# Two levels of an HGRN head's score matrix from products on VectorE and matrices of ones on TensorE

## What is computed

```
def hgrn2_chunk_scan(q, k, v, log_f):
    b = jnp.cumsum(log_f, axis=2)
    diff = b[:, :, :, None] - b[:, :, None, :]
    dec = jnp.where(mask, jnp.exp(jnp.where(mask, diff, 0.0)), 0.0)
    att = jnp.einsum('bnthk,bnshk,bntshk->bnhts', q, k, dec)
    o_intra = jnp.einsum('bnhts,bnshv->bnthv', att, v)
...
    o = hgrn2_chunk_scan(qh, k_f, vh, a_f) + \
        flip(hgrn2_chunk_scan(flip(qh), flip(k_b), flip(vh), flip(a_b)))
```

## Time and profile before

| | |
|---|---|
| median of 3 runs | 1494.94 us |
| profiled execution | 1494.7 us |
| its span | 1492.9 us |
| TensorE (PE) busy | 1468.7 us, 98%, 11148 matmul records |
| VectorE (DVE) busy | 1069.0 us, 72% |
| ScalarE (ACT) busy | 803.8 us, 54% |
| granted TensorE clock | 0.997 of full speed |
| share of the chain that ended last on TensorE | 95% |

### The profile page before, as it was taken

The page is one execution under the profiler, slowest core; times in us unless marked ns, Lnnn a source line. Parts: engine busy times, 40 slices in busy tenths (PEclk is TensorE's granted clock), DMA queues, the critical chain, the costliest instruction groups (busy, mean ns, idle before and its releaser), DMA issues.

```text
span 1492.9 us, 27955 instructions
## 1 busy us (share of the span) xinstructions
PE 1468.7 (98%) x11148; PEld 1397.0 (94%) x11148; DVE 1069.0 (72%) x1818; ACT 803.8 (54%) x1721; POOL 90.6 (6%) x109
## 2 busy tenths in 40 slices
PE   7999999999999999999999999999999999999996
PEld 7999999999999999999999999999998889999984
DVE  7777777777664777777677777777786657777755
ACT  6555545655434555665555555556554446655542
POOL 0000000000000000000000000000001000000100
PEclk9999999999999999999999999999999999999998
DMA  5112111111213222222132121212112232222221
GB/s 208 60 55 71 58 58 57 58 57 58 86 58 100 73 72 72 72 72 72 57 100 85 59 69 59 70 57 71 57 58 86 71 100 72 74 84 79 79 78 64
DMA packets 34625, 109.94 MB, mean 74 GB/s; under 512 B 4928, under 2 KB 5056, under 8 KB 34496
## 3 DMA queue, kind: packets, MB, share of 16 engines
q1 hardware_dynamic: 34496, 108.15, 23.1%
HBM read 97.38 MB, written 2.10 MB: 67 GB/s over the span
## 4 chain that ended last, share of the span: by engine, by line
PE 95%; DVE 2%; ACT 1%; issue 1%; DMA 0%; DVEq 0%; SPq 0%; ACTq 0%
PE proj L1441 66%; PE pair L1510 8%; PE meta L1620 4%; PE pair L1605 2%; PE pair L1607 2%; PE main L1634 2%; PE meta L1622 1%; PE main L1575 1%; PE main L1576 1%; PE pair L1556 1%; PE main L1488 1%; PE main L1517 1%; PE pair L1563 1%; PE main L1579 1%; PE pair L1542 0%
## 5 line engine op out<-in xcount | busy, mean ns | idle before, releaser
L1441 PE MATMUL proj<-u_hi,w_hi 128*128 128x264 f32 (+1 forms) x2048 | 495.3, 313 | 8.7 <-DVE w_lo L1003 7.8
L1441 PE MATMUL proj<-u_hi,w_lo 128*128 128x264 f32 (+1 forms) x2048 | 465.6, 299 | 0.0
L1441 PE MATMUL proj<-u_lo,w_hi 128*128 128x264 f32 (+1 forms) x2048 | 465.5, 299 | 0.0
L1441 PEld LDWEIGHTS proj<-u_hi,w_hi 128*128 128x128 f32 x2048 | 327.2, 190 | 21.2 <-DVE w_lo L1003 7.8
L1441 PEld LDWEIGHTS proj<-u_hi,w_lo 128*128 128x128 f32 x2048 | 326.3, 189 | 11.2
L1441 PEld LDWEIGHTS proj<-u_lo,w_hi 128*128 128x128 f32 x2048 | 326.7, 189 | 7.8
L1003 DVE TENSOR_TENSOR w_lo<-w_raw,w_hi 128x1024 fp32r<-128x1024 f32 x178 | 219.0, 1231 | 49.5 <-ACT w_hi L648 49.3
L648 ACT ACTIVATE w_hi<-w_raw 128x1024 fp32r<-128x1024 f32 x178 | 186.7, 1050 | 64.3 <-PE proj L1441 62.6
L839 ACT ACTIVATE decay<-pair,neg_max 128x528 f32<-128x528 f32 (+1 forms) x144 | 100.3, 697 | 218.4 <-DVE neg_max L1319 218.3
L1319 DVE TENSOR_REDUCE neg_max<-pair 128x1 f32<-128x528 f32 (+1 forms) x144 | 101.5, 705 | 110.6 <-PE pair L1607 110.5
L771 ACT ACTIVATE q_level<-ops 128x528 f32<-128x528 f32 (+1 forms) x112 | 76.5, 683 | 86.0 <-DVE ops L1221 85.8
(11 more groups left out here) (183 smaller groups left out, 2175.2 us busy)
## 6 DMA issues: line engine op xcount, KB each, us to landing
w_raw<-w_units SPq DMA_DIRECT2D x178, 512.0 KB, 3.5
q_stack<-gate_f SPq DMA_DIRECT2D x32, 132.0 KB, 2.4
k_stack<-k_stack SPq DMA_DIRECT2D x32, 132.0 KB, 2.4
h<-x_t SPq DMA_DIRECT2D x8, 264.0 KB, 5.1
cos_sin<-rope SPq DMA_DIRECT2D x2, 528.0 KB, 6.0
out_t<-decay SPq DMA_DIRECT2D x4, 256.0 KB, 2.1
out_t<-ops SPq DMA_DIRECT2D x4, 256.0 KB, 2.1
masks<-level_masks SPq DMA_DIRECT2D x1, 448.0 KB, 5.9
```

Of the source, the lines that this page charges most:

```text
L1441: ins = pe.matmul(out, w, x[:, tile, cols_n], start=(k == 0 and p == 0), stop=(k == last_k and p == 2))
```

## The change

Level 0 and level 1 are no longer matmuls of keys by queries. VectorE makes elementwise products of keys and queries: `own_dots` at step 0 (each token with itself) and `next_dots` at step 1 (each token with its neighbour in the pair), both into `dots`, a part of `decay` with 2 rows of 528. ScalarE rounds `dots` to its high part `dots_hi` (`raise_dots`, in `q_stack`), VectorE subtracts for the low part `dots_lo` (`cut_dots`, in `k_stack`). TensorE then sums over the channels with `parity` as the stationary matrix, whose columns are ones for even tokens (row 0) or odd ones (row 1): 4 fp32r matmuls of 512 columns into one bank of `pair`, and in the first layer 4 more of 16x16 for the meta tokens, before each of the wide ones. That result holds both levels in their places, so ScalarE copies it whole and VectorE's masked copy of level 1 goes. TensorE has nothing of the head at step 1 and does `near_level` at step 2. The copies of keys and queries for level 1 go from ScalarE. `parity` is made at the start by a memset on GpSimd, on which ScalarE waits before its first instruction, and two copies on ScalarE.

```
+            pool.memset(parity[:, :, :].bitcast(f32), 0.0).then_inc(pads_set, 1)
...
             def copy_diagonal(g):
-                act.wait_ge(level_done, g * LEVELS + 1)
-                act.activation(score[:, :, :], pair[:, 0, :].rearrange("p (c n) -> p c n", c=N_CHUNKS),
+                act.wait_ge(level_done, products_done(g, 1))
+                act.activation(score[:, :, :], pair[:, 1, :].rearrange("p (c n) -> p c n", c=N_CHUNKS),
                                ACT.Copy).then_inc(level_read, 1)
+            def raise_dots(g):
+                act.wait_ge(dots_ready, 2 * (g + 1))
+                act.activation(dots_hi[:, :, :], dots, ACT.Copy).then_inc(dots_raised, 1)
...
             def hgrn(l, c, s):
-                if s == 0:
-                    copy_keys(g, c, 1)
-                    copy_queries(g, c, 1)
                 if s == 1:
-                    copy_diagonal(g)
+                    raise_dots(g)
                 if 2 <= s <= TURNS:
                     copy_keys(g, c, s)
                     copy_queries(g, c, s)
+                if s == 2:
+                    copy_diagonal(g)
...
-            act.wait_ge(pads_set, 5)
+            act.wait_ge(pads_set, 6)
             load_root_table()
+            step(act.activation(parity[:, 0, :].rearrange("p (n h) -> p n h", h=2)[:, :, 0], ones[:, 0:P // 2], ACT.Copy))
+            act.activation(parity[:, 1, :].rearrange("p (n h) -> p n h", h=2)[:, :, 1], ones[:, 0:P // 2], ACT.Copy)\
+                .then_inc(parity_set, 1)
...
                 dve.tensor_tensor(ops[:, c % 2, QF, :], q_raw, gate_f[:, 0, :], ALU.mult)\
                     .then_inc(qk_ready, 1)
+                dve.tensor_tensor(own_dots(), k_sum.rearrange("p (b h) -> p b h", h=2),
+                                  q_raw.rearrange("p (b h) -> p b h", h=2), ALU.mult).then_inc(dots_ready, 1)
+            def face_keys(g, c):
...
+                dve.tensor_tensor(next_dots(), keys, queries, ALU.mult).then_inc(dots_ready, 1)
+            def cut_dots(g):
+                dve.wait_ge(dots_raised, g + 1)
+                dve.tensor_tensor(dots_lo[:, :, :], dots, dots_hi[:, :, :].bitcast(f32), ALU.subtract)\
+                    .then_inc(dots_cut, 1)
...
                 elif s == 1:
+                    face_keys(g, c)
                     widen_keys(g, c, 1)
                     total_pairs(1)
+                    cut_dots(g)
                 elif s <= LEVELS:
                     lv = s - 1
                     widen_queries(g, c, lv)
                     if lv < TURNS:
                         widen_keys(g, c, lv + 1)
-                    copy_level(g, lv)
+                    if lv > 1:
+                        copy_level(g, lv)
...
+            def near_level(l, g):
+                if g == 0:
+                    pe.wait_ge(parity_set, 1)
+                pe.wait_ge(dots_cut, g + 1)
+                for part, x in enumerate((dots_hi, dots_lo)):
+                    for row in range(2):
+                        first, last = part + row == 0, part + row == 2
+                        if l < LAST:
+                            pe.matmul(meta[0:N_META, N_META:2 * N_META], parity[:, row, 0:N_META],
+                                      x[:, row, 0:N_META], start=first, stop=last)
+                        ins = pe.matmul(pair[:, 1, :], parity[:, row, :], x[:, row, N_META:T],
+                                        start=first, stop=last)
+                ins.then_inc(level_done, 1)
```

More of the change, by code:

```diff
@@ L106 @@
 TURNS = LEVELS - 1
+PRODUCTS = LEVELS - 1
+COPIES = LEVELS - 2
 READY = LEVELS + 1
@@ L340, in encoder_trunk @@
         qk_dec = sb("qk_dec", [P, 2, 2, T])
+        dots = decay[:, 0:2, :]
         q_raw = qk_dec[:, 1, 0, :]
@@ L343, in encoder_trunk @@
         k_level = qk_dec[:, 0, :, :]
+        parity = sb("parity", [P, 2, P], f32r)
         q_level = sb("q_level", [P, 2, T])
@@ L397, in encoder_trunk @@
         k_widened = sem("k_widened")
+        parity_set = sem("parity_set")
+        dots_ready = sem("dots_ready")
+        dots_raised = sem("dots_raised")
+        dots_cut = sem("dots_cut")
         k_copied = sem("k_copied")
@@ L537, in moved_halves, with own_dots, next_dots, products_done @@
             return bass.AP(tensor=whole.tensor, offset=whole.offset, ap=[part, half, blocks, one])
+        def own_dots():
+            at = dots[:, 0, :]
+            return bass.AP(tensor=at.tensor, offset=at.offset, ap=[at.ap[0], [2, T // 2], [T + 1, 2]])
+        def next_dots():
+            at = dots[:, 0, :]
+            return bass.AP(tensor=at.tensor, offset=at.offset + 1, ap=[at.ap[0], [2, T // 2], [T - 1, 2]])
+        def products_done(g, lv):
+            return g * PRODUCTS + lv
         def facing_totals(m, first):
@@ L1166, in copy_meta_levels @@
             def copy_meta_levels(g):
-                dve.wait_ge(level_done, g * LEVELS + META_LEVELS)
-                w = step(dve.tensor_copy(score_meta[0:N_META, 0:N_META], meta[0:N_META, 0:N_META]))
-                for lv in range(1, META_LEVELS):
+                dve.wait_ge(level_done, products_done(g, META_LEVELS - 1))
+                w = step(dve.tensor_copy(score_meta[0:N_META, 0:N_META], meta[0:N_META, N_META:2 * N_META]))
+                for lv in range(2, META_LEVELS):
                     after(w)
@@ L1193, in start_operands @@
                 dve.wait_ge(k_scaled, 2 * (g + 1))
+                if g > 0:
+                    dve.wait_ge(dots_raised, g)
                 dve.tensor_tensor(k_sum, ops[:, c % 2, KF, :], ops[:, c % 2, KB, :], ALU.add)\
                     .then_inc(qk_ready, 1)
+                dve.wait_ge(qk_ready, g * READY + 1)
                 t = l * LAYER_UNITS + FIRST_UNIT[c] + 2
@@ L1505, in level @@
+            def level(l, g, c, lv):
+                if lv >= 3:
+                    pe.wait_ge(level_read, products_done(g, lv - 2))
+                pe.wait_ge(k_copied, g * COPIES + lv - 1)
+                pe.wait_ge(q_copied, g * COPIES + lv - 1)
                 if lv < META_LEVELS and l < LAST:
-                    k, q = operands(0, N_META)
-                    pe.matmul(meta[0:N_META, lv * N_META:(lv + 1) * N_META], k, q, start=True, stop=True)
+                    pe.matmul(meta[0:N_META, lv * N_META:(lv + 1) * N_META], k_level[:, lv % 2, 0:N_META],
+                              q_level[:, lv % 2, 0:N_META], start=True, stop=True)
@@ L1508, in level @@
                 for j in range(N_CHUNKS):
-                    k, q = operands(N_META + j * P, P)
-                    ins = pe.matmul(pair[:, lv % 2, j * P:(j + 1) * P], k, q, start=True, stop=True)
+                    ins = pe.matmul(pair[:, lv % 2, j * P:(j + 1) * P], k_level[:, lv % 2, chunk(j)],
+                                    q_level[:, lv % 2, chunk(j)], start=True, stop=True)
                 ins.then_inc(level_done, 1)
@@ L1527, in hgrn @@
                 n, g = l * HEADS + c, l * HG_HEADS + c
-                if 1 <= s <= LEVELS:
-                    if s == 1 and n > 0:
-                        pe.wait_ge(o_taken, n)
+                if 2 <= s <= LEVELS:
+                    if s == 2:
+                        if n > 0:
+                            pe.wait_ge(o_taken, n)
                         if c > 0:
                             pe.wait_ge(states_ready, g)
-                    level(l, g, c, s - 1)
+                        near_level(l, g)
+                    else:
+                        level(l, g, c, s - 1)
                     if s == LEVELS:
```

48 lines of the change are left out of this document (21 added, 27 removed).

## The result

The changed kernel takes 1508.7 us (median of 4: 1506.8 to 1510.6) where the kernel before takes 1495.0 beside it: 1.0091 times as long, with a 95% interval of 1.0077 to 1.0104. Its profiled execution took 1507.17 us, 12.5 more than that of before. I forecast 1496.9 and a range up to 1499.6. The result lies far outside, on the slow side.

What follows compares the result with a forecast made beforehand. The prediction took TensorE, busy 98% of the span, as the bound. Its work of -10.4 us and new waits of +12.5 gave +2.1, taken as +2.0, so 1496.9 us against 1494.94, range 1492.0 to 1499.6.

Steps and rivals of the forecast that it cites:

- The products: VectorE's elementwise products of keys and queries at steps 0 and 1, expected to take 0.7 us each.
- The rival on slow products: VectorE's strided products take twice the time, 1.4 us, adding 7.6 us for 1504.5 us; chance 0.1.
- let `own_dots` vanish in VectorE's idle time: own_dots falls into the 0.79 or 1.59 us in which VectorE waits for the next unit.
- The narrow matmuls: Four 16x16 matmuls between the wide ones in layer 0 cost TensorE 0.275 us each, 1.10 a head.
- the rival that I gave 0.25: The 16x16 matmuls are nearly free, 0.12 us each, taking 4.2 us off for 1492.7 us; chance 0.25.
- TensorE's work alone: TensorE's matmul time without waits changes by -0.45 us a head in layer 0, -0.85 in layer 1, -10.4 in all.
- The waits in ordinary heads: TensorE's new wait for cut_dots before near_level at step 2: 0.68 us a head in layer 0, 0.52 in layer 1.
- both heads 0: First head of each layer: products stand behind cut_low, so TensorE waits 1.93 us in layer 0, 2.14 in layer 1.
- Heads 2 and 7: Counted among the seven ordinary heads of each layer, with waits of 0.68 us in layer 0 and 0.52 in layer 1.
- No wait at steps 3 or 4: TensorE waits for nothing at steps 3 or 4 though VectorE's cut_low and widen_queries slip by some 0.6 us.
- the signs that I had named for being wrong: Layer 0's heads get shorter, TensorE waits less than 0.3 us a head, or a wait shows at steps 3 or 4.
- the sizes that I had named as its signs: About 12 us new TensorE idle time, 0.7 us products, layer 0 wide matmuls 0.5 us apart, rounding right behind cut_high.

Runs made afterwards that it cites:

- run 3: Changed kernel with own_dots writing swapped neighbours in one row and face_keys writing alternately to columns 16 bytes apart, output differs; no total time given.
- run 8: The run 5 kernel with three of the four 16x16 matmuls of near_level left out in layer 0, output differs a little; 1479.72 us.
- run 5: Run 1 kernel with face_keys, raise_dots, cut_dots and level 1's widen_keys and widen_queries moved earlier, scale_tables to step 8 of head 2; 1482.4 us, 0.9915 times before.
- run 1: Changed kernel with the loops of both products turned, so each writes all of one row of dots before the other; 1499.8 us, 1.003 times before.
- run 9: Run 1 kernel with scale_tables moved from step 0 of heads 2 to their step 8; 1497.6 us.
- run 2: Changed kernel with near_level multiplying the long-ready u_hi and u_lo, and TensorE waiting for dots_cut a step later, output differs; 1491.15 us.
- run 7: Changed kernel with face_keys put ahead of cut_low at the two heads 0 only; 1503.95 us.
- run 10: Run 5 kernel with cut_dots carried out three times over, so that TensorE waits before near_level in every head; 1541.2 us.
- run 11: Run 5 kernel with cut_dots carried out four times over, for longer waits of TensorE; 1570.1 us.

## Why the prediction was wrong

**The products** are the step that failed. I priced them at 0.7 us, by plain rows and `widen_keys`, and gave their being slow one chance in ten. They take 1.13 and 1.15. `widen_keys` has no write that jumps between two rows from element to element, so it was no row for this. With the loops turned they take 0.70 and 8.9 of the 11.8 us between forecast and result are gone: in the profiles 7.0 of idle time, and 1.6 for one fall of the clock fewer.

The rival on slow products had the mechanism. That its price of 7.6 us comes near is luck. It took twice 0.7, 1.4 us. For products 0.45 us longer the same working gives 0.03 in a head of layer 0, 0.38 in one of layer 1 and 0.4 at heads 0, 3.7 in all, and the waits grew by 7.0. I had let `own_dots` vanish in VectorE's idle time; run 3 shows that in layer 0 it doesn't, and at heads 2 both products are paid, 0.8 us each.

**The narrow matmuls** I priced at 0.275 and they cost 0.11 (run 8), so that the rival that I gave 0.25 was right at the same time: 32 x 0.165 is 5.3 us in the kernel's favour. The forecast took the row of a float32 pair, 75 ns apart with a gap ahead, for fp32r. TensorE's work alone fell by 1.10 and 0.86 a head, 15.7 us in all, not 10.4, as run 5's heads show. Here the page that I cited against my value, "TensorE: Matmul & The Clock Gate" of the Trainium skill, was nearer than my row.

**The waits in ordinary heads** came near where the products are quick. I had counted them from the moment at which TensorE's next matmul would start without a wait. Counted so, run 1 has 0.86 us in layer 0 and 0.54 in layer 1, against 0.68 and 0.52, and 2.23 at both heads 0, against 1.93 and 2.14. In layer 0 the forecast had 0.05 us from the end of `cut_dots` to TensorE's start, and it is 0.15, as it is in layer 1, where I had counted the first load. The idle time that the profile gives, 0.70 and 0.39, is 0.16 less each time, because it begins at the end of a record, and a group's records last 0.41 us where the next start is due after 0.25. Run 5, head 3 of layer 0, has that start without a wait:

```profile
177.16 0.41 PE L1496 MATMUL proj<-u_hi,w_lo 128*128 128x264 f32 x2
177.41 0.17 PE L1555 MATMUL meta<-q_stack,parity 128*16 128x16 f32 x1
```

In layer 1 the four matmuls behind the wait also take 1.00 us up to the next group in place of 0.93. That closes the sum: a head of layer 0 should add -1.10 + 0.86 = -0.24 and adds -0.24, one of layer 1 -0.86 + 0.54 + 0.07 = -0.25 and adds -0.25.

**Heads 2 and 7** I took for ordinary ones. In run 1 head 2 waits 1.56 and 0.75, since `scale_tables` stands in the chain; run 9 shows it and puts 1.2 us on it. Head 7 waits 1.43 and 1.24 us. In the trace before, most of its first levels lie 2.7 us apart in layer 0 where the others' lie 3.4, so TensorE has fewer pieces to do and comes sooner. That this is the cause is read from the spacing; no run tried it.

**The clock** I left out. Before the change TensorE never waits in an HGRN head, and its clock does not fall there. Two falls cost 3.2 us in the changed kernel's profile. Two of its other executions, at a mean clock of 0.993, are 3.4 us longer than the other two; by the same price that is two more falls, but they have no trace.

These account for the difference. The changed kernel's profile: -15.7 of TensorE's work, +21.5 of idle time and 16 x 0.16 = +2.6 that the idle time leaves out, 8 x 0.07 = +0.6 behind the waits of layer 1, +3.2 for the clock, together +12.2, where 12.5 was measured.

Run 1 is the kernel that I had forecast, and there errors cancel. It is 3.7 us over the kernel before in the profiles, where I had 2.0. But that is -15.7 of TensorE's work, +17.2 of waits as I had counted them, +0.6 behind those of layer 1 and +1.6 for one fall of the clock, and not -10.4 + 12.5: TensorE's work was 5.3 us less than I thought and the waits about as much more.

"No wait at steps 3 or 4" was right for the change, but only because it was late already: when run 2 took the first wait away, the one for the queries was there. Of the signs that I had named for being wrong, none came true (but for head 1 of layer 0, shorter by 0.10 us), and still the forecast was. What did miss were the sizes that I had named as its signs: 21.5 us of idle time for 12, products of 1.13 for 0.7, wide matmuls 0.345 apart in layer 0 for 0.5, a rounding that waits. I had written no sign for longer products but their duration, and none for a wait too long.

What stays open is what moving ScalarE's rounding ahead of its cut alone would give; it was only moved along with `face_keys`, `cut_dots` and `scale_tables`.

## What to carry to other kernels

When two results are interleaved into two buffers, let the inner loop stay in one of them, and put the jump on the operand that is read if it must be somewhere; price an access pattern only by a row that writes in the same order. Work that leaves the bounding engine pays only if the chain that feeds its replacement starts early enough on the other engines, and behind the first wait there may be a second: put a ready operand in, as run 2 did, and see which wait is next. Then look at heads or stages one by one, as special instructions and shorter steps make the worst waits, and a wait of two us on TensorE may cost another 1.6 in its clock.

## What the runs showed of the hardware

- A VectorE product of two float32 operands with 528 results per partition takes 0.70 us, with its inner loop of two as without, where writes go to every column or every second one, or swap neighbours. It takes 1.13 to 1.16 when they alternate between columns 16 bytes or a row apart. Reads that do so take 0.72 (one operand, 16 bytes) and 0.85 (both, a row).
- TensorE's granted clock halves, from 2.4 to 1.2 GHz, behind some waits of 1.6 to 2.5 us inside a busy stretch, and not behind others of the same length: in the profiles of the change and of runs 1, 2, 3, 7 and 9 it fell behind 8 of the 21 waits of 1.5 us or more (in run 3 behind 2.01 and 1.59 and not behind 2.49 and 2.51), and 2.34 went both ways in run 10. In no profile did it fall behind a wait of 1.4 us or less in a head; it fell behind 13 of 16 of 2.0 to 3.3 us and behind 15 of 16 of 3.3 to 4.6. A fall lasted 3.4 us and cost 1.6; six of the 15 in run 11 lasted longer. Executions spread with it: the changed kernel's, at mean clocks of 0.995 and 0.993, are 3.8 us apart, those of run 5, all at 0.997, 0.9.
- A 16x16 fp32r matmul between wide ones costs TensorE 0.11 us. A wait in front of `near_level` costs 0.16 us more than the idle time that the profile gives, which begins only at the end of the last record, and in layer 1 0.07 more behind it.
